# Value products of the prompt attention as two fp32r products of split operands, with the weighing on GpSimd

## The chip, the cores and the metric

The kernel runs on one core of a Trainium2 chip. The metric is the time of one execution on the device in microseconds (us); three executions of the kernel before took 1511.27, 1512.11 and 1513.88 us, the median is 1512.11.

TensorE is called PE in the profile, VectorE DVE, ScalarE ACT, GpSimd POOL and SyncE SP.

## The reference, cut to what matters

One layer of a decoder for a prompt of 1024 positions and, beside it, 8 x 4 sampled positions: a convolution, a pooling group and a sparse attention work side by side on 1024 features, then comes a feed-forward part. The change touches the attention of the prompt alone. It has 8 query heads in 2 groups (one key and value head per group, 64 features each) and three branches: compressed, selected and window, each with its own keys and values. For 1024 positions the selected branch comes down to all earlier positions; the window is 512 positions.

```python
    s = jnp.einsum('bqgrd,bgqmd->bgrqm', q, kg).astype(jnp.float32) * scale + bias
    p = masked_softmax(s, (dist >= 0)[:, :, None])
    o_slc = jnp.einsum('bgrqm,bgqmd->bqgrd', p.astype(vg.dtype), vg)
...
    p = masked_softmax(s, mask)
    o_win = jnp.einsum('bgrqk,bkgd->bqgrd', p.astype(vw.dtype), vw)
    return o_cmp, o_slc, o_win

def gate_sum(gates, o_cmp, o_slc, o_win):
    return gates[:, :, 0] * o_cmp + gates[:, :, 1] * o_slc + gates[:, :, 2] * o_win
```

All of it is fp32.

## The kernel before, in words

The program is one launch, with a hand-written instruction stream for every engine and semaphores between them. The stages follow each other: projection and convolution, the attention of the sampled positions, the attention of the prompt, output projection, feed-forward. The attention of the prompt runs from its first score product at 344.5 us to its last value product at 616.6 us.

There the work goes over 8 tiles of 128 queries (i = 0 to 7). Each tile has five groups in the order of the list ORDER: selected and window for the first head group (g = 0), the compressed branch for both, selected and window for the second (g = 1). A group of the selected or window branch is called dense; it has four heads (r = 0 to 3) and covers up to 1024 keys (selected) or 640 (window). The generator steps() sets the order of every engine: for each dense group q and each head r it yields the score jobs to issue and some of the turned tiles (128 keys, 4 heads) of the group three earlier (a lag of three groups). So the scores of one group, its exponentials, its weighing and its value products lie far apart in the program, and every engine walks the same list.

Of one step:

- TensorE makes the scores of a head into psA or psB (p_score, L1017 and L1018, fp32r, two products per 512 columns, one with the rounded queries and one with their rests). Then, per tile of the older group, it turns the weighed probabilities of four heads (four transposes of 128 x 128, L731) into a turn bank and makes the value product of the tile two before (p_values, L1037): an fp32 product of 512 columns into bank 6, whose 64 useful rows for g stand in one half, with zeros beside the values for the other half. Bank 6 collects all five groups of a query tile.
- VectorE adds the bias and takes the maximum of the job's scores (p_biased_max, L1814 to L1820), makes a group's four weights (reciprocal of the sum times the gate, group_weights, L1858 and L1861) once per group, and weighs one head of an older group (weigh_head, L1867: up to 1024 columns times one number per query, in place). The compressed branch has its own operations (c_center, L1834 and L1835; c_scale).
- ScalarE makes the exponentials of the jobs of the step before (L1415), copies every turned tile from its bank to probT (three slots, L1312), and copies bank 6 out to featT once per query tile (out_tile, L1421).
- GpSimd copies and pads the values of the prompt before the stage starts, and splits keys (L2143, L2144) and queries (L2146, L2150) into a rounded part and a rest, which the queue of SyncE copies to their places for the score products (L649).

The turned tiles go round three banks (4, 5, 7; turn_bank, turn_free): TensorE may turn tile u once tile u - 3 was copied out.

At the stage's end ScalarE copies out the last output (L1421), rounds the eight feature tiles (L1457), VectorE makes their rests (L1909), and TensorE goes on with the output projection (L1094). Rounded parts and rests of that projection's first two weight tiles are made before, at the tail of the attention (round_w on ScalarE, rest_w on VectorE, L1884).

Of the kernel before, what the change touches and what calls it, by code (L numbers as in the profile page):

```python
# [21 lines left out]
P = 128  # L22
D = 1024
# [220 lines left out]
def turn_bank(u):  # L244

    if U_C <= u < U_C + 2 * NB:
        return 4 + (u - U_C) % 4
    return 4 + u % 2 if u < U_T else (4, 5, 7)[(u - U_T) % 3]


def turn_free(u):

    if U_C <= u < U_C + 2 * NB:
        return u - 4 if u >= U_C + 4 else U_C - 1
    if U_C + 2 * NB <= u < U_C + 2 * NB + 2:
        return U_C + 2 * NB - 1
    return u - 2 if u < U_T else U_T - 1 if u < U_T + 3 else u - 3


OUT_AFTER = {i: max(u for k, u in PUNIT.items() if k[0] == "t" and GROUPS[k[1]][0] == i) for i in range(NT)}  # L260
# [23 lines left out]
def build(nc, A, out):  # L284
    ctx = ExitStack()
    with ctx:
# [84 lines left out]
        probT = [probTb[:, k, :] for k in range(NPT)]  # L371
        cmpw = at("cmpw", [P, 3, 8, P], 168960)
# [40 lines left out]
        def page_slot(pj, b):  # L413
# [39 lines left out]
            "gate_mm gate_ev qbd_done score_mm score_in exp_done sum_read cmp_scaled turn_drain_d probT_used keys_used out_done rec_done scaled o_ev v_pad split_done k_in q_in0 q_in1 q_in2 prob_zero "  # L453
            "x2_in0 x2_in1 x_pad mixH_done mixL_done raw_in0 raw_in1 wH_done wL_done unit_mm third_mm out_ev rest_ev "
            "acc_done moment_mm sd_done inv_done t_done silu_done up_scaled hid_done aH_done aL_done y_add gain2_in gain3_in "
# [17 lines left out]
        def wait_drained(eng, key):  # L473

            if key in DRAINED_D:
# [40 lines left out]
        def _(sp):  # L516
# [179 lines left out]
            def load_gu(f, w):  # L696
                if isinstance(f, int) and f == 1:
                    sp.wait_ge(s["acc_done"], 1)
                    sp.wait_ge(s["rest_ev"], 3 * KD)
                    sp.dma_start(gB[:, :], A["final_norm"][None, :].to_broadcast([P, D])).then_inc(s["gain3_in"], 16)  # L700
# [27 lines left out]
        def _(pe):  # L728
# [292 lines left out]
            def p_values(n, x):  # L1021

                i, g, br = GROUPS[n]
                pt = probT[PUNIT[("t", n, x)] % NPT]
                wait_drained(pe, ("t", n, x))
                o = bank[6]
                if br == 0:
                    mm = pe.matmul(o, vcBD, pt, start=False, stop=False)
                else:
                    first = x == 0 and (g, br) == ORDER[0]  # L1030
                    if first and i == 0:
                        pe.wait_ge(s["v_pad"], 4)
                    elif first:
                        pe.wait_ge(s["o_ev"], i)
# [172 lines left out]
        def _(sc_):  # L1207
# [224 lines left out]
            for _, _, jobs, tiles in steps():  # L1432
# [3 lines left out]
                for n, x in tiles:  # L1436
# [5 lines left out]
                    if key not in DRAINED_D:  # L1442
                        sc_.wait_ge(s["probT_used"], pu - NPT + 1)
                        drain(key, [(probT[pu % NPT], lambda b: b)])
                    else:
                        nturn[0] += 1
                    for o, last in OUT_AFTER.items():
                        if last == pu - 2:
                            out_tile(o)
            out_tile(NT - 1)  # L1450
# [3 lines left out]
            for k in range(KD):  # L1454
                if k == 4:
                    sc_.wait_ge(s["o_ev"], NT)
# [76 lines left out]
        def _(dve):  # L1533
# [335 lines left out]
            def turn_copy(key):  # L1869

                pu = PUNIT[key]
                dve.wait_ge(s["turn_fill"], UNIT[key] + 1)
                dve.wait_ge(s["probT_used"], pu - NPT + 1)
                dve.tensor_copy(probT[pu % NPT], bank[4 + UNIT[key] % 2]).then_inc(s["turn_drain_d"], 1)
# [12 lines left out]
            for q, r, jobs, tiles in steps():  # L1887
# [6 lines left out]
                if 0 <= old < len(DG):  # L1894
                    if head == 0:
                        group_weights(DG[old])
                    weigh_head(DG[old], head)
                if r == 3 and rider(q) is not None:
                    c_scale(rider(q))
                for n, x in tiles:  # L1900
                    if ("t", n, x) in DRAINED_D:
                        turn_copy(("t", n, x))
# [101 lines left out]
            dve.wait_ge(s["gain3_in"], 16)  # L2004
# [16 lines left out]
        def _(pool):  # L2021
# [213 lines left out]
```

## Time and profile before

| | |
|---|---|
| median of 3 executions | 1512.11 us (1511.27 to 1513.88) |
| the profiled execution | 1512.36 us |
| its span | 1510.2 us |
| mean granted TensorE clock of the span | 0.987 |
| TensorE / VectorE busy | 1451.0 / 759.1 us |
| ScalarE / GpSimd busy | 477.7 / 219.2 us |
| attention of the prompt | 344.5 to 616.6 us |

The span goes from the first to the last instruction of the profiled execution; the execution's own time is 2.2 us longer. Busy times of an engine are sums over its instructions' records; records of one engine overlap a little, since an instruction starts before the one ahead has left the pipeline. PEclk is the granted clock of TensorE in a stretch (1.00 is 2.4 GHz, 0.50 is 1.2 GHz). A line L731 stands for the operation that helper records, whatever the tile.

### The profile page before, as it was taken

What the parts mean: (1) busy time and instruction counts of PE and PEld (TensorE: products, weight loads), DVE (VectorE), ACT (ScalarE), POOL (GpSimd) and SP (SyncE); (2) the same over time, 40 slices, a digit from 0 to 9 for tenths busy, and PEclk for the clock granted to TensorE, in tenths of its full rate; (3) what the DMA queues carried; (4) which work ended last, traced back from release to release, by engine and by line L of the source; (5) the groups of instructions that cost most, each with busy time, mean ns of one, the idle gap of its engine ahead of it and who ended that gap; (6) DMA issues with size and microseconds to landing.
All of it is one profiled execution on the core that took longest, in us unless ns stands there. A gap on an engine that the chain in (4) does not pass through costs nothing.

```text
span 1510.2 us, 22117 instructions
## 1 busy us (share of the span) xinstructions
PE 1451.0 (96%) x8743; PEld 1330.9 (88%) x8743; DVE 759.1 (50%) x1535; ACT 477.7 (32%) x961; POOL 219.2 (15%) x251
## 2 busy tenths in 40 slices
PE   6999999888999999899999999999999999999996
PEld 6999988656666666699999999999999999999996
DVE  5499933226887776322424443524253344435257
ACT  5122124236776666422311211211121112111123
POOL 2114102520000000044220101010100101010105
PEclk9999999999999999999999999999999999999998
DMA  8731114943111102232110211202020202112012
GB/s 204 192 78 30 45 31 125 303 112 77 43 28 29 29 1 43 55 87 74 54 46 22 63 39 50 63 26 73 11 74 19 70 22 64 42 46 67 18 49 115
DMA packets 165815, 98.98 MB, mean 66 GB/s; under 512 B 35650, under 2 KB 160537, under 8 KB 165633
## 3 DMA queue, kind: packets, MB, share of 16 engines
q1 hardware_dynamic: 163217, 88.71, 21.5%
q0 software_dynamic: 2496, 8.88, 2.2%
q8 instruction: 69, 1.13, 0.3%
q14 instruction: 33, 0.27, 0.1%
HBM read 78.33 MB, written 13.19 MB: 61 GB/s over the span
## 4 chain that ended last, share of the span: by engine, by line
PE 82%; DVE 7%; SPq 3%; DMA 3%; ACT 2%; issue 2%; POOL 0%; POOLq 0%; DVEq 0%; ACTq 0%
PE psA L1065 16%; PE psB L1065 16%; PE psC L1065 16%; PE psD L1037 6%; PE psC L731 4%; DVE ybuf L1653 4%; DMA zraw<-in_w_in 2%; PE psD L731 2%; PE psA L782 2%; PE psA L1094 2%; PE psB L1094 2%; PE psC L1094 2%; PE psB L782 2%; PE psC L782 2%; PE psB L1017 1%
## 5 line engine op out<-in xcount | busy, mean ns | idle before, releaser
L1429 ACT CAST wH<-wraw 128x1024 fp32r<-128x1024 f32 (+1 forms) x132 | 86.7, 658 | 262.2 <-PE psC L1065 176.4
L2174 POOL TENSOR_TENSOR hid<-hid,rstdB 128x352 f32<-128x352 f32 x66 | 74.8, 1162 | 629.1 <-ACT hid L1490 629.1
L1037 PE MATMUL psD<-probTb,kvtok 128*128 128x512 f32 x264 | 135.7, 597 | 2.2 <-ACT featT L1421 2.1
L1884 DVE TENSOR_TENSOR wL<-wraw,wH 128x1024 fp32r<-128x1024 f32 (+1 forms) x132 | 107.2, 813 | 44.7 <-ACT wH L1429 44.7
L1065 PE MATMUL psA<-gH,wH 128*128 128x352 f32 x352 | 113.7, 323 | 0.0
L1065 PE MATMUL psB<-gH,wH 128*128 128x352 f32 x352 | 113.7, 323 | 0.0
L1065 PE MATMUL psC<-gH,wH 128*128 128x352 f32 x352 | 113.5, 322 | 0.0
L1065 PE MATMUL psA<-gH,wL 128*128 128x352 f32 x352 | 113.2, 322 | 0.0
L1065 PE MATMUL psB<-gH,wL 128*128 128x352 f32 x352 | 113.1, 321 | 0.0
L1065 PE MATMUL psA<-gL,wH 128*128 128x352 f32 x352 | 113.1, 321 | 0.0
L1065 PE MATMUL psB<-gL,wH 128*128 128x352 f32 x352 | 112.9, 321 | 0.0
L1065 PE MATMUL psC<-gL,wH 128*128 128x352 f32 x352 | 112.8, 321 | 0.0
L1065 PE MATMUL psC<-gH,wL 128*128 128x352 f32 x352 | 112.8, 320 | 0.0
L1653 DVE SCALAR_TENSOR_TENSOR ybuf<-glu,convw,ybuf 128x1296 f32<-128x1296 f32 x60 | 103.3, 1766 | 0.7
L1939 DVE TENSOR_TENSOR hid<-psA,rstdB 128x352 f32<-128x352 f32 x44 | 21.0, 520 | 160.7 <-PE psB L1065 160.6
L1947 DVE TENSOR_TENSOR hid<-psB,hid 128x352 f32<-128x352 f32 x22 | 11.5, 525 | 167.4 <-PE psC L1065 167.4
L1490 ACT ACTIVATE hid<-hid 128x352 f32<-128x352 f32 x66 | 29.9, 499 | 204.9 <-DVE hid L1939 204.9
L1312 ACT COPY probTb<-psC 128x512 f32<-128x512 f32 (+2 forms) x104 | 58.8, 565 | 46.7 <-PE psC L731 46.4
L1494 ACT CAST aH<-hid 128x352 fp32r<-128x352 f32 x66 | 31.5, 487 | 122.8 <-DVE hid L1947 121.8
L1065 PEld LDWEIGHTS psA<-gL,wH 128*128 128x128 f32 x352 | 66.4, 189 | 0.0
L1065 PEld LDWEIGHTS psB<-gH,wL 128*128 128x128 f32 x352 | 66.2, 188 | 0.0
L1065 PEld LDWEIGHTS psA<-gH,wH 128*128 128x128 f32 x352 | 66.0, 188 | 0.2
(426 smaller groups left out, 3898.7 us busy)
## 6 DMA issues: line engine op xcount, KB each, us to landing
wraw<-in_w_gu SPq DMA_DIRECT2D x44, 512.0 KB
wraw<-in_w_down SPq DMA_DIRECT2D x80, 128.0 KB
zraw<-in_w_in SPq DMA_DIRECT2D x12, 512.0 KB
xa<-in_x_prompt SPq DMA_DIRECT2D x8, 512.0 KB, 8.4
pages<-in_cache_cmp_kv SPq DMA_DIRECT2D x32, 128.0 KB, 2.4
qS<-qH SPq DMA_DIRECT2D x32, 128.0 KB, 2.4
qS<-qL SPq DMA_DIRECT2D x32, 128.0 KB, 2.4
xs<-in_x_prompt SPq DMA_DIRECT2D x8, 512.0 KB, 3.8
```

The lines of the kernel that those rows point to most:

```text
L731: return pe.transpose(dst, src, ident[0:n, 0:n])
L782: mm = pe.matmul(bank[3 * (m % 2) + n][:, 0:w], wt[:, m % 2, k, :], mv[:, k, c0:c0 + w], start=(k == 0 and wt is zH and mv is xH), stop=(k ...
L1037: mm = pe.matmul(o, kvtok[:, kt, vc:vc + P], pt, start=first, stop=((g, br) == ORDER[-1] and x == len(g_tiles(n)) - 1))
L1065: mm = pe.matmul(bank[3 * par + n][:, 0:cw], wt[:, par, k, :], mv[:, k, at:at + cw], start=(k == 0 and mv is mH and wt is wH), stop=(k == ...
L1094: mm = pe.matmul(b[:, 0:cw], wt[:, par, k, :], mv[:, k, c0:c0 + cw], start=False, stop=(k == KD - 1 and wt is wL))
L1312: op = sc_.copy(dst, srcfn(bank[turn_bank(u)]))
L1429: sc_.copy(wH[:, par, 0:nk, :], wraw[:, par, 0:nk, :]).then_inc(s["wH_done"], 1)
L1490: sc_.activation(hid[:, n, :], hid[:, n, :], ACT.Silu).then_inc(s["silu_done"], 1)
L1494: sc_.copy(aH[:, par, x // 2, at:at + cw], hid[:, n, :]).then_inc(s["aH_done"], 1)
L1653: op = dve.scalar_tensor_tensor(out=y, in0=x, scalar=w, in1=y, op0=ALU.mult, op1=ALU.add)
L1884: dve.tensor_tensor(wL[:, par, 0:nk, :], wraw[:, par, 0:nk, :], wH[:, par, 0:nk, :].bitcast(F32), ALU.subtract).then_inc(s["wL_done"], 1)
L2174: pool.tensor_tensor(hid[:, n, :], hid[:, n, :], rstdB[:, c0:c0 + cw], ALU.mult).then_inc(s["up_scaled"], 1)
```

## The change

It touches the value products and all that feeds them.

- The probabilities are kept as a rounded part and a rest: ScalarE's copy of a turned tile now rounds to fp32r (probH), and VectorE subtracts that from the bank (rest_tile, L1881: probL). TensorE's next turn into that bank, and the tile's value products, wait for this rest (semaphore pl_done).
- The values are split, too, by GpSimd: a tile vS holds for each key tile, branch and head group the 64 rounded columns and the 64 columns of rests side by side. One product with vS thus gives rounded and rest values in the two halves of the bank's rows. p_values makes two fp32r products per tile, with probH (L1048) and with probL (L1049).
- The outputs of g = 0 collect in bank 6 and those of g = 1 in bank 7, so there are two turn banks (4, 5) for the tiles. The compressed tile becomes two fp32 products over 64 rows each, one into bank 6 and one into bank 7.
- The two halves of a bank have to be added: ScalarE copies one half to featT (out_half, twice per query tile), VectorE adds the other (out_sum, L1889).
- The weighing of the probabilities moves from VectorE to GpSimd (L2184), group by group when the weights are there (rec_done).
- GpSimd's two padding copies and memsets of the values go; in their place stand 32 casts and 32 subtractions of 64 columns, each waiting for the one before, ahead of the split of the keys.
- Two semaphores are new (pl_done, o_half), one is folded into another (gain3_in into gain2_in).

```diff
@@ turn_bank, turn_free @@
-    return 4 + u % 2 if u < U_T else (4, 5, 7)[(u - U_T) % 3]
+    return 4 + u % 2
...
-    return u - 2 if u < U_T else U_T - 1 if u < U_T + 3 else u - 3
+    return u - 2
@@ wait_drained @@
+            if key in DENSE_T:
+                eng.wait_ge(s["pl_done"], DENSE_T[key] + 1)
@@ p_values @@
-                o = bank[6]
                 if br == 0:
-                    mm = pe.matmul(o, vcBD, pt, start=False, stop=False)
+                    if i:
+                        pe.wait_ge(s["o_ev"], 2 * i)
+                    pt = probT[slot]
+                    pe.matmul(bank[6], vcBD[0:HD, :], pt[0:HD, :], start=False, stop=False)
+                    mm = pe.matmul(bank[7], vcBD[HD:P, :], pt[HD:P, :], start=True, stop=False)
                 else:
...
-                    mm = pe.matmul(o, kvtok[:, kt, vc:vc + P], pt, start=first,
-                                   stop=((g, br) == ORDER[-1] and x == len(g_tiles(n)) - 1))
+                    last = br == 2 and x == len(g_tiles(n)) - 1
+                    pe.matmul(bank[6 + g], vS[:, kt, vc:vc + P], probH[:, slot, :], start=first, stop=False)
+                    mm = pe.matmul(bank[6 + g], vS[:, kt, vc:vc + P], probL[slot][:, :], start=False, stop=last)
@@ ScalarE @@
-            def out_tile(i):
-
-                sc_.wait_ge(s["probT_used"], OUT_AFTER[i] + 1)
-                sc_.copy(featT[:, 4:8, P * i:P * i + P], bank[6].rearrange("p (r t) -> p r t", r=GQ)
-                         ).then_inc(s["o_ev"], 1)
+            def out_half(i, g):
+
+                sc_.wait_ge(s["probT_used"], OUT_AFTER[i, g] + 1)
+                gp, other = slice(HD * g, HD * g + HD), slice(HD * (1 - g), HD * (1 - g) + HD)
+                sc_.copy(featT[gp, 4:8, P * i:P * i + P], bank[6 + g][other, :].rearrange("p (r t) -> p r t", r=GQ)
+                         ).then_inc(s["o_half"], 1)
...
-                        drain(key, [(probT[pu % NPT], lambda b: b)])
+                        drain(key, [(probH[:, pu % NPT, :] if n in DENSE else probT[pu % NPT], lambda b: b)])
@@ VectorE @@
-            def weigh_head(n, r):
-
-                p = prob(n, r)[:, 0:g_width(n)]
-                dve.tensor_scalar(p, p, precs[DENSE[n] % 4][:, r:r + 1], None, ALU.mult).then_inc(s["scaled"], 1)
...
+            def rest_tile(n, x):
+
+                key = ("t", n, x)
+                slot = PUNIT[key] % NPT
+                dve.wait_ge(s["turn_drain"], DRAINED_A[key])
+                dve.tensor_tensor(probL[slot][:, :], bank[turn_bank(UNIT[key])], probH[:, slot, :].bitcast(F32), ALU.subtract
+                                  ).then_inc(s["pl_done"], 1)
+
+            def out_sum(i, g):
+
+                gp = slice(HD * g, HD * g + HD)
+                o = featT[gp, 4:8, P * i:P * i + P]
+                dve.wait_ge(s["o_half"], 2 * i + g + 1)
+                dve.tensor_tensor(o, bank[6 + g][gp, :].rearrange("p (r t) -> p r t", r=GQ), o, ALU.add).then_inc(s["o_ev"], 1)
...
-                    weigh_head(DG[old], head)
...
+                    if n in DENSE:
+                        rest_tile(n, x)
+                    for o, last in OUT_AFTER.items():
+                        if last == PUNIT["t", n, x] - 4:
+                            out_sum(*o)
+            out_sum(NT - 1, 1)
             for w in range(2):
                 rest_w(w, w, KD)
@@ GpSimd @@
-            for br in (1, 2):
-                c = 256 * br
-                pool.tensor_copy(kvtok[:, 0:NT, c:c + HD], kvtok[:, 0:NT, c + P:c + P + HD]).then_inc(s["v_pad"], 1)
-            for br in (1, 2):
-                c = 256 * br
-                pool.wait_ge(s["v_pad"], br)
-                pool.memset(kvtok[:, 0:NT, c + HD:c + HD + P], 0.0).then_inc(s["v_pad"], 1)
...
+            for i in range(NT):
+                for br in (1, 2):
+                    c = 256 * br
+                    for g in range(KVH):
+                        v = kvtok[:, i, c + P + HD * g:c + P + HD * g + HD]
+                        vh = vS[:, i, c + P * g:c + P * g + HD]
+                        pad(pool.tensor_copy(vh, v))
+                        pad(pool.tensor_tensor(vS[:, i, c + P * g + HD:c + P * g + P], v, vh.bitcast(F32), ALU.subtract))
...
+            for q, n in enumerate(DG):
+                pool.wait_ge(s["rec_done"], q + 1)
+                for r in range(GQ):
+                    p = prob(n, r)[:, 0:g_width(n)]
+                    pool.tensor_scalar(p, p, precs[q % 4][:, r:r + 1], None, ALU.mult).then_inc(s["scaled"], 1)
```

The order of TensorE's instructions, before: one head of the last query tile, with two tiles of an older group (psC holds the turn banks 4 and 5, psD the banks 6 and 7; narrow and wide are the probabilities of window and selected groups).

```order
L1018 MATMUL psA<-kS,qS_111 128x320
L731 MATMUL psC<-cpk,wide 128x128 [waits turn_drain]
L731 MATMUL psC<-cpk,wide 128x128 x3
L1037 MATMUL psD<-probTb,kvtok 128x512 [waits turn_drain]
L731 MATMUL psC<-cpk,wide 128x128 [waits turn_drain]
L731 MATMUL psC<-cpk,wide 128x128 x3
L1037 MATMUL psD<-probTb,kvtok 128x512 [waits turn_drain]
L1017 MATMUL psB<-kS,qS_111 128x320 [waits exp_done]
```

And of the change, at the same place.

```order
L1025 MATMUL psA<-kS,qS_116 128x320
L738 MATMUL psC<-cpk,wide 128x128 [waits pl_done]
L738 MATMUL psC<-cpk,wide 128x128 x3
L1048 MATMUL psD<-probH,vS 128x512 [waits pl_done]
L1049 MATMUL psD<-probL_107,vS 128x512
L738 MATMUL psC<-cpk,wide 128x128 [waits pl_done]
L738 MATMUL psC<-cpk,wide 128x128 x3
L1048 MATMUL psD<-probH,vS 128x512 [waits pl_done]
L1049 MATMUL psD<-probL_105,vS 128x512
L1024 MATMUL psB<-kS,qS_116 128x320 [waits exp_done]
```

The places of transposes and value products are the same; both now wait for VectorE's rest (pl_done) where they waited for ScalarE's copy (turn_drain).

The order of VectorE's instructions in a step of the same stretch, before.

```order
L1814 TENSOR_TENSOR psB<-psB,tri 128x128 [waits score_mm]
L1818 TENSOR_REDUCE small_115<-psB 128x1 [waits dve]
L1820 ISA psB,nmax<-psB,btab,small_115 128x256 [waits exp_done,dve]
L1820 ISA nmax 128x1
L1867 TENSOR_SCALAR narrow<-narrow,small_115 128x640
```

And of the change.

```order
L1826 TENSOR_TENSOR psB<-psB,tri 128x128 [waits score_mm]
L1830 TENSOR_REDUCE small_120<-psB 128x1 [waits dve]
L1832 ISA psB,nmax<-psB,btab,small_120 128x256 [waits exp_done,dve]
L1832 ISA nmax 128x1
L1881 TENSOR_TENSOR probL_105<-psC,probH 128x512 [waits turn_drain]
L1881 TENSOR_TENSOR probL_106<-psC,probH 128x512 [waits turn_drain]
```

The weighing behind a maximum is gone, and the rests of the step's tiles (one or two) stand there, each waiting for ScalarE's copy.

VectorE at the end of the stage, before.

```order
L1861 TENSOR_TENSOR small_115<-small_115,kvtok 128x4 [waits sum_read]
L1867 TENSOR_SCALAR narrow<-narrow,small_115 128x640 [waits rec_done]
L1867 TENSOR_SCALAR narrow<-narrow,small_115 128x640 x3
L1884 TENSOR_TENSOR wL<-wraw,wH 128x1024 [waits wH_done] x2
L1909 TENSOR_TENSOR fL<-featT,fH 128x1056 [waits mixH_done] x8
```

And of the change.

```order
L1881 TENSOR_TENSOR probL_106<-psC,probH 128x512 [waits turn_drain]
L1881 TENSOR_TENSOR probL_107<-psC,probH 128x512 [waits turn_drain]
L1889 TENSOR_TENSOR featT<-psD,featT 64x4x128 [waits o_half]
L1899 TENSOR_TENSOR wL<-wraw,wH 128x1024 [waits wH_done] x2
L1927 TENSOR_TENSOR fL<-featT,fH 128x1056 [waits mixH_done] x8
```

The rests of the two weight tiles now stand behind the last tile's rest and the last half sum of the stage.

## Rows read from the trace of the kernel before

**Rows 1.** The page, busy times and shares of the span by engine:

```profile
PE 1451.0 (96%) x8743; PEld 1330.9 (88%) x8743; DVE 759.1 (50%) x1535; ACT 477.7 (32%) x961; POOL 219.2 (15%) x251
```

**Rows 2.** Windows of the stage (stretch, its length, busy by engine, PEclk, DMA share, GB/s):

```profile
371.80:588.90 217.10, 210.46 (x1042) 146.07 (x1042) 172.88 (x509) 149.51 (x319) 0.21 (x1) 1.00 0.10 25
588.90:616.60 27.70, 27.70 (x126) 16.20 (x125) 6.12 (x12) 14.13 (x25) 0.00 (x0) 1.00 0.29 58
```

**Rows 3.** Timeline of TensorE (start, us), and the page's group of value products:

```profile
542.67 0.40 PE L1018 MATMUL psB<-kS,qS 128*128 128x512 f32 x1
542.91 0.60 PE L731 MATMUL psD<-cpk,narrow 128*128 128x128 f32 x4
543.34 1.02 PE L1037 MATMUL psD<-probTb,kvtok 128*128 128x512 f32 x2
544.20 0.60 PE L731 MATMUL psC<-cpk,narrow 128*128 128x128 f32 x4
...
L1037 PE MATMUL psD<-probTb,kvtok 128*128 128x512 f32 x264 | 135.7, 597 | 2.2 <-ACT featT L1421 2.1
```

**Rows 4.** Timeline of VectorE, and the long part's window for L1867 alone (DVE busy):

```profile
559.92 0.69 DVE L1835 TENSOR_TENSOR psB<-psB,small 128x504 f32<-128x504 f32 x1
560.52 0.17 DVE L1858 RECIPROCAL small<-small 128x4 f32<-128x4 f32 x1
...
371.80:588.90 217.10, 50.92 (x95) 1.00 0.10 25
```

**Rows 5.** Timelines of GpSimd and SyncE's queue; groups of GpSimd by line:

```profile
290.03 1.89 POOL L2143 CAST keysH<-keysT 128x2048 fp32r<-128x2048 f32 x1
292.00 4.52 POOL L2144 TENSOR_TENSOR keysT<-keysT,keysH 128x2048 fp32r<-128x2048 f32 x1
296.47 3.59 POOL L2146 CAST qH<-qT 128x4096 fp32r<-128x4096 f32 x1
321.65 1.81 SPq L649 DMA_DIRECT2D kS<-keysH  x3
...
L2150 POOL TENSOR_TENSOR qL<-qT,qH 128x512 fp32r<-128x512 f32 x8 | 9.8, 1264 | 31.6 <-PE psD L974 31.6
L2174 POOL TENSOR_TENSOR hid<-hid,rstdB 128x352 f32<-128x352 f32 x66 | 74.8, 1162 | 629.1 <-ACT hid L1490 629.1
```

**Rows 6.** Timelines of TensorE and ScalarE in the tail:

```profile
588.72 0.60 PE L731 MATMUL psC<-cpk,wide 128*128 128x128 f32 x4
608.18 0.60 PE L731 MATMUL psC<-cpk,narrow 128*128 128x128 f32 x4
608.88 0.59 ACT L1312 COPY probTb<-psC 128x512 f32<-128x512 f32 x1 [0.71 <-PE psC L731]
613.38 0.60 PE L731 MATMUL psC<-cpk,narrow 128*128 128x128 f32 x4
```

**Rows 7.** The chain that ended last in order of time; VectorE's timeline:

```profile
616.59 0.59 ACT featT L1421
617.17 0.98 ACT fH L1457
618.18 9.46 DVE fL L1909 x8
627.68 0.79 PE psA L1094 x3
...
598.76 2.36 DVE L1884 TENSOR_TENSOR wL<-wraw,wH 128x1024 fp32r<-128x1024 f32 x2 [5.59 <-ACT wH L1429]
```

**Rows 8.** Windows around two low clocks (the first two: transposes alone, PE and PEld):

```profile
252.34:255.75 3.41, 3.41 (x16) 2.65 (x15) 0.50 0.80 229
255.75:270.00 14.25, 12.75 (x105) 11.05 (x103) 1.00 0.77 227
...
347.91:351.33 3.42, 2.04 (x14) 1.51 (x12) 3.00 (x20) 1.08 (x5) 0.00 (x0) 1.00 0.36 88
351.33:354.74 3.41, 2.83 (x13) 2.73 (x14) 2.98 (x22) 2.90 (x13) 0.00 (x0) 0.50 0.27 68
```

More of the change, by code:

```diff
@@ L256, in turn_free @@
         return U_C + 2 * NB - 1
-    return u - 2 if u < U_T else U_T - 1 if u < U_T + 3 else u - 3
-OUT_AFTER = {i: max(u for k, u in PUNIT.items() if k[0] == "t" and GROUPS[k[1]][0] == i) for i in range(NT)}
+    return u - 2
+OUT_AFTER = {(i, g): max(u for k, u in PUNIT.items() if k[0] == "t" and GROUPS[k[1]][:2] == (i, g))
+             for i in range(NT) for g in range(KVH)}
+DENSE_T = {k: m for m, k in enumerate([k for k in PUNIT if k[0] == "t" and k[1] in DENSE])}
 LASTQ = [(n, m) for n in range(3) for m in range(KD)]
@@ L371, in build @@
         probT = [probTb[:, k, :] for k in range(NPT)]
+        probH = at("probH", [P, NPT, 512], 158720, F32R)
+        probL = [at(f"probL{k}", [P, 512], o, F32R) for k, o in enumerate((54528, 164864, M_S + 2528))]
+        vS = at("vS", [P, NT + 1, KVG], M_Z, F32R)
         cmpw = at("cmpw", [P, 3, 8, P], 168960)
@@ L452, in build @@
             "late_zero turn_fill turn_drain page_in0 page_in1 page_in2 page_in3 cmpw_in0 cmpw_in1 cmpw_in2 cmpw_used cmp_half cmp_sum cmp_ev posr_in "
-            "gate_mm gate_ev qbd_done score_mm score_in exp_done sum_read cmp_scaled turn_drain_d probT_used keys_used out_done rec_done scaled o_ev v_pad split_done k_in q_in0 q_in1 q_in2 prob_zero "
+            "gate_mm gate_ev qbd_done score_mm score_in exp_done sum_read cmp_scaled turn_drain_d probT_used keys_used out_done rec_done scaled pl_done o_half o_ev v_pad split_done k_in q_in0 q_in1 q_in2 prob_zero "
             "x2_in0 x2_in1 x_pad mixH_done mixL_done raw_in0 raw_in1 wH_done wL_done unit_mm third_mm out_ev rest_ev "
-            "acc_done moment_mm sd_done inv_done t_done silu_done up_scaled hid_done aH_done aL_done y_add gain2_in gain3_in "
+            "acc_done moment_mm sd_done inv_done t_done silu_done up_scaled hid_done aH_done aL_done y_add gain2_in "
             "lraw_in0 lraw_in1 lH_done lL_done last_mm y_last back_turn x_add sq_y accf_done ms3 rstd3 y_done_d y_done_a y_out").split()
@@ L473, in wait_drained @@
         def wait_drained(eng, key):
-            if key in DRAINED_D:
+            if key in DENSE_T:
+                eng.wait_ge(s["pl_done"], DENSE_T[key] + 1)
+            elif key in DRAINED_D:
                 eng.wait_ge(s["turn_drain_d"], DRAINED_D[key])
@@ L1448, in _ @@
                         if last == pu - 2:
-                            out_tile(o)
-            out_tile(NT - 1)
+                            out_half(*o)
+            out_half(NT - 1, 1)
             sc_.wait_ge(s["stores"], 16 * STORES)
@@ L1455, in _ @@
                 if k == 4:
-                    sc_.wait_ge(s["o_ev"], NT)
+                    sc_.wait_ge(s["o_ev"], 2 * NT)
                 sc_.copy(fH[:, k, :], featT[:, k, :]).then_inc(s["mixH_done"], 1)
@@ L1862, in group_weights @@
                 dve.wait_ge(s["rec_done"], q + 1)
-            def weigh_head(n, r):
-                p = prob(n, r)[:, 0:g_width(n)]
-                dve.tensor_scalar(p, p, precs[DENSE[n] % 4][:, r:r + 1], None, ALU.mult).then_inc(s["scaled"], 1)
[L1869 to L1874, printed above, removed]
+            def rest_tile(n, x):
[9 more added lines that the diff above has]
+                dve.tensor_tensor(o, bank[6 + g][gp, :].rearrange("p (r t) -> p r t", r=GQ), o, ALU.add).then_inc(s["o_ev"], 1)
             def link2(op):
@@ L2002, in last_scale @@
                                       ).then_inc(s["y_done_d"], 1)
-            dve.wait_ge(s["gain3_in"], 16)
+            dve.wait_ge(s["gain2_in"], 32)
             for q, turns in last_steps():
@@ L2140, in in_turn, with pad @@
                 pool.wait_ge(s["pool"], count[0])
+            pads = [0]
+            def pad(op):
+                pads[0] += 1
+                op.then_inc(s["v_pad"], 1)
+                pool.wait_ge(s["v_pad"], pads[0])
+            for i in range(NT):
[6 more added lines that the diff above has]
+                        pad(pool.tensor_tensor(vS[:, i, c + P * g + HD:c + P * g + P], v, vh.bitcast(F32), ALU.subtract))
             old = slice(0, T)
```

12 lines of the change are left out of this document (5 added, 7 removed).

## The prediction

> **What bounds the kernel now.** The page's busy shares come first: TensorE is busy 96% of the span and VectorE 50% [rows 1], so an edit that only shortens VectorE would be worth nothing on average. But these are averages over the whole program, and the change touches one stage, so the windows come next. The attention of the prompt runs from 344.5 us (first score product) to 616.6 us (last value product). In its long part, 371.8 to 588.9 us, TensorE is busy 210.46 of 217.10 us and VectorE 172.88 [rows 2]: TensorE is the bound, VectorE follows at 80%. The 27.7 us after that hold no scores, only the last three groups' tiles: TensorE is busy throughout, VectorE for 6.12 us. Then come 11 us in which TensorE waits for the rests of the features [rows 7]. GpSimd does nothing in the stage but one memset. So I read two limits: what TensorE gives back, and how close VectorE is behind it.
>
> **What a tile costs TensorE.** In the timeline four transposes start at 542.91 and the value product behind them at 543.34: 0.43 us. The next transposes start at 544.20: the fp32 value product, which the trace shows as two passes of 512 columns, holds TensorE for 0.86 us. A score product, fp32r with 512 columns, starts at 542.67 and the next instruction at 542.91: 0.24 us [rows 3]. The change puts two fp32r products of 512 columns where one fp32 product was: 2 x 0.24 = 0.48 instead of 0.86, 0.38 us less per tile. There are 132 tiles of the selected and window branches (x264 passes), so 50 us less for TensorE, 114 x 0.38 = 43 us of it in the long part: 210.5 - 43 = 167 us of work there. The compressed tiles (8) become two products of 64 rows each; even at twice 0.86 they add 7 us to an engine that then has 40 us to spare. I cost them at nothing.
>
> **What VectorE gets.** Removed: the weighing, 95 instructions and 50.92 us of records in the long part. Records overlap: an operation of 504 columns from PSUM starts at 559.92, is recorded with 0.69 us, and the next one starts at 560.52, 0.60 later [rows 4]. With 0.08 us of overlap each, the weighing frees 50.9 - 95 x 0.08 = 43 us. Added: one subtraction per tile (128 x 512, PSUM minus SBUF), nearest to that row of 504 columns, so 0.605 us of the queue: 114 x 0.605 = 69 us, and the two half sums of each query tile, same form, 14 x 0.605 = 8.5 us. VectorE in the long part: 172.9 - 43 + 69 + 8.5 = 207.4 us. That is more than TensorE's 167: **VectorE becomes the bound**, and of the 43 us that TensorE gives back at most 217.1 - 207.4 = 9.7 can show. What remains is idle time of VectorE. TensorE, as the bound with three turn banks, was idle 217.1 - 210.5 = 6.6 us. Now there are two turn banks, a bank comes free only when VectorE has subtracted, and a subtraction at the head of VectorE's queue holds back the next score's maximum. Against that, ScalarE (some 150 us of the long part, plus eight half copies) and TensorE have 50 and 40 us of slack. I take 5 us of idle, between 0 (gain 9.7) and 10 (gain nothing): **-4.7 us**. The short first part (344.5 to 371.8, small tiles, waiting on each other rather than on throughput) gets one more link per tile: +0.5.
>
> **GpSimd.** It takes over the weighing. The trace has no such operation there. From below: a cast of 2048 columns took 1.89 us, 0.92 ns a column; from above: a product of two inputs in the feed-forward part, 352 columns in 1162 ns, 3.3 ns a column [rows 5]. The widest query tile (four groups, 8 x 1024 + 8 x 640 = 13,312 columns) then costs 12 to 44 us of GpSimd per some 45 us, and its result is wanted nearly two groups later. One input is nearer to the cast, so I take 0.92 and cost it at nothing; the cover is the lag of three groups. The Trainium skill's GPSIMD Engine Reference (§ 4.1 Engine selection) calls GpSimd about two times slower than VectorE for operations of two inputs and roughly line-rate for one; the two rows agree with that, and it points to the lower end.
>
> GpSimd also splits the values into 64 small casts and subtractions that wait on each other, ahead of the keys' split, in place of two copies and two memsets. Casts of 2048 and 4096 columns took 1.89 and 3.59 us, so 0.19 fixed and 0.83 ns a column: 0.25 us for 64 columns; subtractions of 512 and 2048 columns took 1.26 and 4.52, so 0.32 for 64. With 0.08 between dependent ones (the cast that starts 290.03 and ends 291.92, the next at 292.00) it is 32 x (0.33 + 0.40) = 23 us. The keys' split ended at 296.5 and would end at 320; the DMA queue asks for it at 321.65, after its own wait for TensorE [rows 5]. Hidden, by 2 us.
>
> **The tail.** Now the first transposes of the part start at 588.72 and the last at 613.38, 19 steps of 1.30 us, and the end comes 3.2 us later [rows 6]. After the change TensorE needs 0.43 + 0.48 = 0.91, but the ring through two banks is longer: transposes 0.60, ScalarE's start 0.10 behind (608.78 to 608.88), its copy 0.59, 0.10, subtraction 0.69, 0.10: 2.18 us for two tiles, 1.09 each. So 19 x 1.09 + 2.18 + 0.67 (last two products and their drain) = 23.6 against 27.9: **-4.3 us**.
>
> **The end of the stage.** From 616.59 the chain is: copy of the last output 0.59, rounding of the features, their rests on VectorE 9.46, and TensorE goes on at 627.68 [rows 7]. In the new order of VectorE the last half sum stands ahead of the rests of the first two weight tiles (2.36 us, now done at 598.76 in the idle tail), and these ahead of the feature rests. So 0.59 + 0.05 + 0.69 + 0.05 + 2.36 + 0.05 + 9.46 = 13.2 instead of 11.1: **+2.1 us**.
>
> **Sum.** -4.7 + 0.5 - 4.3 + 2.1 = -6.4 us. The profiled execution took 1512.36 us (span 1510.2), 0.25 above the median of 1512.11; against the median this gives 1505.7.
>
> **Rivals.**
> *VectorE runs packed* (chance 0.08): the rests fall into its idle time, no more is lost than semaphores. For: VectorE's records already lie close in narrow steps. Gain 9.7 + 4.3 - 2.1 = 12: 1500.
> *Half the gain is lost to the ring* (0.15): 10 us of idle instead of 5, and a ring of 1.15: 1510 to 1513, no change.
> *VectorE's queue is blocked* (0.10), the case on the other side: in 22 steps of the long part two tiles stand behind one maximum. If the second subtraction there waits for one copy of ScalarE (0.59), since its bank came free only with the subtraction before, that is 13 us: 1505.7 + 13 = 1519. It decides from 0.3 us per such step (6.6 us) on. Against it: while the maximum runs (over 1 us), the copy of the first tile and the transposes of the second fit in.
> *GpSimd is late with the keys* (0.06): at over 0.39 us per small operation (25 us / 64) the key copies move. At 0.62 they start 15 us late, some 5 of which the queue's slack before the first score takes: 1516.
> *GpSimd is late with the weights* (0.03): only above 3.5 ns a column; at 4, 270 us for all 67,584 columns, over 1520.
> *The clock falls* (0.03). TensorE will be busy for 80% of the long part, a good part of it transposes. In the trace it went to 0.50 (1.2 GHz) at 351.33 after 2.04 busy of 3.42 us; and in 252.34:255.75, at 0.50, every record is a transpose, and the stretch behind it has 1.00 [rows 8]. So transposes did not keep the clock down. If it fell for every other such stretch, TensorE would need 167 x 4/3 = 223 instead of 212: 1516. The Trainium skill (TensorE: Matmul & The Clock Gate, Part 4) says that transposes do not count as busy in the same way; by that rule this rival would be likely, but rows 8 speak against it.
>
> **How the numbers follow.** The forecast, 1502 to 1509, has 0.55. A measurement of this kernel tells about 0.2% (3 us) from no change. Faster by more: 0.55 + 0.08 = 0.63. Within: 0.15 and a little of the keys' case, 0.17. Slower: 0.20. The range 1500 to 1516.5 takes in the first three cases and those of the keys and the clock, both 1516; it leaves out 0.13 above and a little below.
>
> **What would show it.** Right: value products at two starts 0.24 apart; TensorE at about 80% and VectorE at over 95% in the long part; waits of TensorE for the subtraction; tiles at 1.09 in the tail; two weight rests between last half sum and feature rests; GpSimd's weighing near 1 ns a column. Wrong: VectorE waiting for ScalarE's copies for more than 10 us in the long part, the first score later than 345 us, TensorE's clock at 0.50 beyond 360 us, or scaled probabilities waited for.

## The result, and the profile after

The changed kernel took 1525.45 us (median of 4 runs, 1524.9 to 1528.06) against 1512.84 for the kernel before (4 runs): a ratio of 1.0088, interval 1.007 to 1.0105. It is 13 us slower, where 6 us faster was forecast; the time lies above the range. The profiled execution took 1525.53 us, its span is 1523.7. One execution of the run with the memset on VectorE (3898.55 us) and one of the kernel before beside it (2074.16) lie far off and are left out of the medians below.

The page's first part of the kernel after answers to [rows 1]: TensorE is busy 31 us less, GpSimd 217 us more.

```profile
PE 1419.9 (93%) x8759; PEld 1328.0 (87%) x8759; DVE 798.9 (52%) x1555; ACT 481.5 (32%) x969; POOL 436.2 (29%) x439
```

The windows of the kernel after answer to [rows 2] (stretch, its length, busy PE, PEld, DVE, ACT, POOL, each with its count, then PEclk, DMA share, GB/s). The first line is the long part; the next two lie in the tail.

```profile
371.80:588.90 217.10, 184.15 (x1044) 143.85 (x1044) 200.13 (x529) 149.87 (x319) 169.15 (x95) 0.98 0.09 23
...
599.80:615.26 15.46, 0.00 (x0) 0.00 (x0) 0.74 (x2) 3.33 (x5) 3.36 (x3) 0.63 0.48 103
615.26:620.45 5.19, 5.18 (x19) 4.29 (x20) 2.52 (x4) 2.06 (x4) 0.00 (x0) 0.50 0.01 3
```

In the tail TensorE stands still for 15.46 us, and for the 5.19 us behind that it runs at the lower clock (0.50). The chain that ended last, of the kernel after in order of time, tells what the pause waits for:

```profile
595.57 7.44 POOL narrow L2184 x4
603.01 0.16 POOL xs L2186
...
603.23 0.37 SPq L680
...
607.98 0.60 SPq L696
608.58 0.04 issue
608.62 4.31 DMA wraw<-in_w_out
...
613.91 0.59 ACT probH L1323
614.49 0.02 issue
614.52 0.70 DVE probL L1881
```

GpSimd finishes the last group's weighing at 603.0; only then comes its memset of the padding rows of the output projection's input (xs). The queue of SyncE waits for that memset before it loads xs, the gain and the first two weight tiles, in this order. The two weight tiles have landed at about 610.8 and 612.9. ScalarE has their rounding (L1441) in its queue ahead of the last two groups' copies, so the copies wait, VectorE's rest behind them, and TensorE's next turn behind that. ScalarE's timeline of the kernel after shows the gap:

```profile
597.29 0.59 ACT L1323 CAST probH<-psC 128x512 fp32r<-128x512 f32 x1 [0.69 <-PE psC L738]
610.86 1.04 ACT L1441 CAST wH<-wraw 128x1024 fp32r<-128x1024 f32 x1 [12.98 <-DMA wraw<-in_w_out]
612.96 1.04 ACT L1441 CAST wH<-wraw 128x1024 fp32r<-128x1024 f32 x1 [1.05 <-DMA wraw<-in_w_out]
```

In the kernel before the same load was issued right behind the last score product (SyncE's timeline of before):

```profile
587.93 0.37 SPq L673 DMA_DIRECT2D xs<-in_x_prompt  x1
```

So the account of the stage, from the two profiled executions: the first score product starts at 343.89 (344.84 before), the last one at 587.25 (587.27): nothing gained up to there. From there to the end of the value products it takes 43.5 us (587.25 to 630.77) instead of 29.3 (587.27 to 616.57): 14.2 more. From there to the last rest of the features 13.1 (to 643.83) instead of 11.1 (to 627.64): 2.0 more. Together 16.2. The span is 13.5 us longer; the other 2.7 come back behind the stage, where the change alters no work. That stretch took 882.6 us before and 879.9 after, and between 878.2 and 881.6 in the runs below, so this part is not put down to the change.

### The profile page after: what moved, and what is told of

It is laid out like the page before. It is cut to its first block, busy times and chain, and to the rows that moved or that the text cites. A ratio compares the mean times of both kernels' runs of the same rounds, so it can differ in the third digit from the quotient of the medians.

```text
span 1523.7 us, 22397 instructions
## 1 busy us (share of the span) xinstructions
PE 1419.9 (93%) x8759; PEld 1328.0 (87%) x8759; DVE 798.9 (52%) x1555; ACT 481.5 (32%) x969; POOL 436.2 (29%) x439
## 4 chain that ended last, share of the span: by engine, by line
PE 76%; DVE 12%; issue 4%; ACT 3%; DMA 2%; POOL 2%; SPq 1%; POOLq 0%; DVEq 0%; ACTq 0%
PE psA L1076 16%; PE psB L1076 16%; PE psC L1076 15%; PE psA L789 4%; PE psB L789 4%; PE psC L789 4%; PE psC L738 3%; DVE small L1830 3%; DVE probL L1881 2%; PE psA L1105 2%; PE psC L1105 2%; PE psB L1105 2%; DVE ybuf L1665 1%; PE psD L738 1%; DVE psB L1832 1%
## 5 line engine op out<-in xcount | busy, mean ns | idle before, releaser
L1441 ACT CAST wH<-wraw 128x1024 fp32r<-128x1024 f32 (+1 forms) x132 | 86.8, 658 | 272.5 <-PE psC L1076 174.0
L2184 POOL TENSOR_SCALAR wide<-wide,small 128x128 f32<-128x128 f32 (+7 forms) x64 | 109.3, 1726 | 33.9 <-DVE small L1873 33.9
L1881 DVE TENSOR_TENSOR probL<-psC,probH 128x512 fp32r<-128x512 f32 x132 | 89.3, 688 | 34.3 <-ACT probH L1323 33.2
L2184 POOL TENSOR_SCALAR narrow<-narrow,small 128x640 f32<-128x640 f32 (+4 forms) x64 | 93.9, 1487 | 25.6 <-DVE small L1873 25.6
L1323 ACT CAST probH<-psC 128x512 fp32r<-128x512 f32 x132 | 76.6, 583 | 38.1 <-PE psC L738 37.3
L738 PE MATMUL psC<-cpk,wide 128*128 128x128 f32 x320 | 51.7, 287 | 22.5 <-DVE probL L1881 22.4
```

The costliest lines, as they stand in the source:

```text
L738: return pe.transpose(dst, src, ident[0:n, 0:n])
L1323: op = sc_.copy(dst, srcfn(bank[turn_bank(u)]))
L1441: sc_.copy(wH[:, par, 0:nk, :], wraw[:, par, 0:nk, :]).then_inc(s["wH_done"], 1)
L1881: dve.tensor_tensor(probL[slot][:, :], bank[turn_bank(UNIT[key])], probH[:, slot, :].bitcast(F32), ALU.subtract).then_inc(s["pl_done"], 1)
L2184: pool.tensor_scalar(p, p, precs[q % 4][:, r:r + 1], None, ALU.mult).then_inc(s["scaled"], 1)
```

## The experiments

Theory Q: the place of one memset in GpSimd's queue makes the pause. Rivals: the weights come late for another reason, or GpSimd's price itself ends the tail. Theory D: VectorE's throughput bounds the long part; its rival R: the ring of two banks does. The medians of the kernel before in the three sets of runs are 1512.24 (first four), 1513.31 (next four) and 1512.67 (the last).

**The memset on VectorE.**

```diff
-            pool.wait_ge(s["score_mm"], NSJ + NJ)
-            pool.memset(xs[0][:, NT, :], 0.0).then_inc(s["x_pad"], 1)
...
+                if (q, r) == (len(DG) - 1, GQ - 1):
+                    dve.memset(xs[0][:, NT, :], 0.0).then_inc(s["x_pad"], 1)
```

> The change as it is, but the one memset that the loads of the output projection's first input and weights wait for is issued by VectorE behind its last maximum, and no longer by GpSimd behind the last weighing. Theory Q (the 15.5 us in which TensorE stands still at 599.8 to 615.3 come from the place of that memset in GpSimd's queue): memset near 588 instead of 603, the weight tiles land near 598, ScalarE's rounding of them no longer holds up the copies of turned tiles, and the slow clock behind the pause goes, too: 1509 us (1507 to 1511). Rival W (the weights come late for a reason of their own, or ScalarE would wait there anyway): the pause stays for the most part, 1518 or more. Rival P (GpSimd's price of 3 ns a column is itself what ends the tail): TensorE then waits for the last group's weighing instead, 1515 to 1520.

Measured: 1513.31 us, ratio 1.0011 (1.0001 to 1.002), 12 us less than the change. Most of the pause is gone and the time lies below what W and P gave, so both fall. 4 us more than expected stay, and VectorE's timeline of this run shows why:

```profile
591.01 0.17 DVE L1909 MEMSET xs<- 128x128 f32 x1
```

And ScalarE's timeline of this run:

```profile
600.79 1.04 ACT L1441 CAST wH<-wraw 128x1024 fp32r<-128x1024 f32 x1 [1.03 <-DMA wraw<-in_w_out]
```

On VectorE the memset has work ahead of it, too, and comes 3 us after the last score product. ScalarE still waits 1.03 us for the second tile, TensorE then 2.40 for the rest behind it, and the low clock follows again.

**The two weight rests off the chain.**

```diff
+            rest_w(0, 0, KD)
             out_sum(NT - 1, 1)
-            for w in range(2):
-                rest_w(w, w, KD)
...
                                   ).then_inc(s["mixL_done"], 1)
+            rest_w(1, 1, KD)
```

> The run before this one, and besides the rest of the first weight tile is made ahead of the last half sum, that of the second behind the rests of the features. The chain behind the last value product then holds no weight rest (2.36 us in the trace of the change): 2.3 us less than the run with the memset alone, about 1507 us. If the two rests were hidden, no difference.

Measured: 1511.05 us, ratio 0.9994 (0.9984 to 1.0004): 2.3 us less than the run before. The time misses the 1507 by the 4 us that were left there; the difference is the one expected. The chain that ended last, of the change:

```profile
631.38 0.69 DVE featT L1889
632.07 0.03 issue
632.10 2.36 DVE wL L1899 x2
634.46 9.36 DVE fL L1927 x8
```

And of this run:

```profile
619.90 0.58 ACT featT L1433
620.50 1.08 ACT fH L1469
621.60 9.45 DVE fL L1928 x8
```

The half sum and the weight rests are no longer on it. This term was forecast as it came out.

**One part alone: the kernel before, with the weighing on GpSimd.**

```diff
-                    weigh_head(DG[old], head)
...
+            for q, n in enumerate(DG):
+                pool.wait_ge(s["rec_done"], q + 1)
+                for r in range(GQ):
+                    p = prob(n, r)[:, 0:g_width(n)]
+                    pool.tensor_scalar(p, p, precs[q % 4][:, r:r + 1], None, ALU.mult).then_inc(s["scaled"], 1)
             pool.wait_ge(s["score_mm"], NSJ + NJ)
             pool.memset(xs[0][:, NT, :], 0.0).then_inc(s["x_pad"], 1)
```

> The kernel before with one part of the change alone: the weighing on GpSimd, ahead of its memset, as the change has it; value product, banks and outputs as before. Theory Q: the long part is bound by TensorE and keeps its length, but the memset comes behind the last weighing, at about 600 instead of 588, so the weights land near 610 where ScalarE wants them near 598: a pause of about 12 us in the tail, 1524 us (1520 to 1527). If the pause comes from the new value products or from the ring of two banks, it isn't here: 1509 to 1513.

Measured: 1524.39 us, ratio 1.0071 (1.0057 to 1.0085). The old value products, three banks, and the same loss. ScalarE's timeline of this run:

```profile
607.07 1.04 ACT L1429 CAST wH<-wraw 128x1024 fp32r<-128x1024 f32 x1 [11.78 <-DMA wraw<-in_w_out]
```

**The same with the memset on VectorE** (the edit of the first run).

> The run before this one with the memset on VectorE behind its last maximum. Theory Q: no pause, and since TensorE bounds the long part, taking 43 us of weighing off VectorE brings next to nothing: 1511 us (1508 to 1513). If GpSimd's weighing at 3 ns a column is late for TensorE's turns, over 1515.

Measured: 1506.19 us, ratio 0.9967 (0.9954 to 0.998). The memset's place alone is worth 18 us between these two runs. And the weighing on GpSimd brings 5 to 6 us by itself, more than expected: from the first score product to the last it takes 238.1 us (345.89 to 584.01) instead of 242.4 (344.84 to 587.27). In the window from 371.8 to the last score product's end, below, TensorE is idle for 3.6 of 212.5 us, where it was for 6.6 of 215.8 up to the same product before (371.8 to 587.58). Of TensorE's waits from 371.8 to 584 two are gone, 2.1 us for ScalarE's copy of bank 6 and 1.1 us for exponentials of selected groups. VectorE is busy for only 133.31 us here; that its queue had held these up before is likely, but not shown.

```profile
371.80:584.30 212.50, 208.91 (x1039) 145.47 (x1038) 133.31 (x412) 148.81 (x318) 171.55 (x98) 1.00 0.10 26
```

**The change with the weighing undone.**

```diff
                     if head == 0:
                         group_weights(DG[old])
+                    wn = DG[old]
+                    wp = prob(wn, head)[:, 0:g_width(wn)]
+                    dve.tensor_scalar(wp, wp, precs[old % 4][:, head:head + 1], None, ALU.mult).then_inc(s["scaled"], 1)
...
-            for q, n in enumerate(DG):
-                pool.wait_ge(s["rec_done"], q + 1)
...
```

> The change with the weighing alone undone (VectorE weighs again, GpSimd's memset then has nothing ahead of it), the two weight rests moved off the chain as in the run with memset and rests, and ScalarE's rounding of the second weight tile one group later. Theory D (VectorE's throughput bounds the long part of the change): 43 us of weighing come on top of 199 us of busy VectorE in 216 us: the long part takes 240 to 250 us, the run 1533 to 1545 us. If VectorE were not the bound (the ring of two banks is), under 1520.

Measured: 1545.53 us, ratio 1.0217 (1.0195 to 1.0238), just above the end of what theory D gave and far from the 1520 of its rival. The window of this run from 371.8 to 621.6 shows VectorE busy for 238.72 of 249.80 us. The last score product ends 3.3 us later, at 624.91, so the long part takes 253.1 us, 3 more than the 250 that were the upper end.

```profile
371.80:621.60 249.80, 193.38 (x1042) 147.60 (x1041) 238.72 (x630) 151.83 (x325) 0.00 (x0) 0.95 0.09 22
```

**The memset early on GpSimd, and the second weight tile rounded later** (the weight rests are moved as in the second run, and the memset behind the weighing is taken out; the cut shows the two new parts).

```diff
             for q, n in enumerate(DG):
+                if q == len(DG) - 2:
+                    for u in range(2 * NT - 3, 2 * NT):
+                        pool.wait_ge(s[f"q_in{u % 3}"], 64 * (u // 3 + 1))
+                    pool.memset(xs[0][:, NT, :], 0.0).then_inc(s["x_pad"], 1)
                 pool.wait_ge(s["rec_done"], q + 1)
...
                     if (n, x) == (NG - 2, 0):
-                        for w in range(2):
-                            round_w(w, w, KD)
+                        round_w(0, 0, KD)
+                    if (n, x) == (NG - 1, 0):
+                        round_w(1, 1, KD)
```

> The change with the memset still on GpSimd, but ahead of the last two groups' weighing (it waits for the last query copies alone), the two weight rests off the chain, and ScalarE's rounding of the second weight tile one group later. Theory Q: loads start with the last score product, no pause is left in the tail (2.4 us and a slow clock behind it were left with the memset on VectorE, where it stood at 591.0): 1507 us (1505 to 1509). If the pause is not the queue's, as the run with memset and rests: 1511.

Measured: 1508.03 us, ratio 0.9964 (0.9951 to 0.9978). This is the change without its mishap, 17 us below it, and 5.3 us below the kernel before. In its trace the tail, from the last score product's start to the end of the value products, takes 26.5 us (591.42 to 617.89), and TensorE's longest wait in it is 0.75 us.

**VectorE relieved, the ring untouched.**

```diff
                 if w > m:
                     least = far[:, job % 2:job % 2 + 1]
-                    link(dve.tensor_reduce(least, sc[:, 0:w - m], AX, ALU.min))
+                    least = 3.0e38
```

> The run with the early memset, and VectorE leaves out the maximum over the keys farther than 256 (95 instructions, some 45 us of its queue in the long part; the exponentials then have a bias from the near keys alone). Nothing of the ring of turned tiles changes. Theory D (throughput): VectorE has 155 us of work left, TensorE 181, the long part goes from 216 to 185-195: 1476 to 1490 us. Theory R (the ring of two banks with the subtraction in it sets the pace): the long part keeps its length within some us, over 1500.

Measured: 1484.76 us, ratio 0.9809 (0.979 to 0.9829), 23 us less than the run with the early memset. It is a probe of VectorE's time and no kernel to keep, since the exponentials lose the maximum over the far keys. The window of this run from 371.8 to the last score product's end:

```profile
371.80:567.80 196.00, 174.31 (x1046) 142.97 (x1046) 152.03 (x440) 150.70 (x325) 171.56 (x99) 1.00 0.11 28
```

And of the run with the early memset:

```profile
371.80:591.70 219.90, 183.63 (x1051) 142.09 (x1049) 201.78 (x535) 151.78 (x326) 171.84 (x100) 0.99 0.10 25
```

VectorE has 49.8 us less to do and the stretch is 23.9 us shorter (1 us above the 185 to 195 expected), with the same two banks. Theory R falls as the cause of the long part's length; the ring is not free either, since only half of what VectorE gave back shows, and now VectorE is idle for 44 us, 30.2 of them in waits for ScalarE's copies of turned tiles. One rival is left open: the run also shortens the way from a job's scores to its exponentials, so by itself it doesn't part VectorE's throughput from that latency. The run with the weighing undone, which adds work behind the maxima and not between scores and exponentials, speaks for throughput.

**Half the tiles split, then two of three.** A tile that is not split keeps its probabilities in fp32 and has no subtraction:

```diff
-DENSE_T = {k: m for m, k in enumerate([k for k in PUNIT if k[0] == "t" and k[1] in DENSE])}
+DENSE_T = {}
+for _j, _k in enumerate([k for k in PUNIT if k[0] == "t" and k[1] in DENSE]):
+    if _j >= 112 or _j % 2:
+        DENSE_T[_k] = len(DENSE_T)
...
+                    else:
+                        mm = pe.matmul(bank[6 + g], vS[:, kt, vc:vc + P].bitcast(F32), probT[slot], start=first, stop=last)
```

> The run with the early memset, but every second tile of the first 112 is not split: its probabilities are copied in fp32 and go through one fp32 product with the same side-by-side values; its subtraction falls away. The last 20 tiles are all split. Theory D: VectorE in the long part 199 - 56 x 0.605 = 165 us, TensorE 181 + 56 x 0.38 = 202: TensorE bounds again, long part 203 to 206 instead of 216: 1495 us (1492 to 1500). If neither VectorE nor TensorE is the bound (GpSimd's weighing, say), 1504 or more.

> The run with half the tiles split, with two of three tiles split among the first 112 (19 more). Theory D: TensorE 200 - 19 x 0.38 = 193 us, VectorE 176 + 19 x 0.605 = 187 us in the long part: nearly level, so the larger falls by 7 us, but both are then close to full and wait for each other: 0 to 5 us less than with half split, 1498 to 1503 us. If VectorE is already the one that waits are made by, more than with half split, up to 1508.

Measured: 1503.47 us, ratio 0.9937 (0.9923 to 0.9951), for half, 3.5 us above its range; the profiled execution of that one was its fastest, 1499.34. 1500.62 us, ratio 0.9924 (0.9907 to 0.994), for two thirds (_j % 3), within its range. The intervals of the two overlap, so which of them is better stays open; both beat the kernel before and the change. The window to the last score product's end, with half:

```profile
371.80:582.10 210.30, 194.67 (x1046) 143.85 (x1045) 172.22 (x477) 149.96 (x321) 169.43 (x97) 0.99 0.10 25
```

And with two thirds:

```profile
371.80:584.00 212.20, 191.93 (x1052) 143.80 (x1050) 184.03 (x500) 152.07 (x325) 171.72 (x100) 0.99 0.10 26
```

The exchange is as the terms say (TensorE down, VectorE up), but the stretch stays at 210 to 212 us, above the 203 to 206 expected of half. Neither engine is full (TensorE is idle for 15.6 and 20.3 us, VectorE for 38 and 28); which of their waits sets the length was not taken apart.

These windows all begin at 371.8, while the first score product starts between 343.9 and 346.4 us in the profiled executions. Counted from the first score product's start to the last one's, the part takes 242.4 us before, 243.4 after, 238.1 with the weighing alone on GpSimd and the memset on VectorE, 245.6 with the early memset (345.81 to 591.42; this execution was the slowest of its run), 237.9 with half split (343.99 to 581.84) and 237.6 with two thirds (346.13 to 583.69). The last score products of the weighing alone and of the run with the early memset:

```profile
584.01 0.31 PE L1018 MATMUL psB<-kS,qS 128*128 128x320 f32 x1
591.42 0.31 PE L1025 MATMUL psB<-kS,qS 128*128 128x320 f32 x1
```

So beside the weighing alone the split of all tiles lengthens this part by 5 to 7 us, and the split of some of them hardly changes it. What the split gives is the tail: 29.3 us before and with the weighing alone, 26.5 with all tiles split and the early memset, 25.6 and 25.8 with half and two thirds. On balance the whole change with the early memset (ratio 0.9964) is no faster than the weighing alone (0.9967).

## Why the prediction was wrong, point by point

**The step that failed is the one on GpSimd**: "I take 0.92 and cost it at nothing; the cover is the lag of three groups". The cover held for those who wait for the weighing itself: TensorE's weight loads waited 1.1 us in all for GpSimd in the stage. But the cover was checked for the weighing alone. What stands behind it in GpSimd's queue, the memset, has a waiter of its own, SyncE's queue of loads, and behind those ScalarE's rounding stands in the queue of the copies. The prediction had read that "GpSimd does nothing in the stage but one memset" [rows 2] and didn't ask who waits for that. The answer was 15.46 us in which TensorE stood still. Shown by the run with the weighing alone (the pause without the new products), most cleanly by its pair, 1524.39 and 1506.19, in which the memset's place alone differs, and by the three places of the memset in the change: 1525.45 behind the weighing, 1511.05 on VectorE (with the weight rests moved), 1508.03 early (with those, and the second weight tile's rounding later). The last link, the rounding in ScalarE's queue ahead of the copies, is read from the program and the traces; no run moved the rounding by itself and left the memset where it was.

**GpSimd's price** was taken near the lower bound and came out near the upper one. Groups by line and shape, GpSimd after:

```profile
L2184 POOL TENSOR_SCALAR narrow<-narrow,small 128x640 f32<-128x640 f32 x32 | 59.8, 1888 | 16.6 <-DVE small L1873 16.6
L2184 POOL TENSOR_SCALAR wide<-wide,small 128x1024 f32<-128x1024 f32 x8 | 22.6, 2848 | 5.1 <-DVE small L1873 5.1
...
L2184 POOL TENSOR_SCALAR wide<-wide,small 128x128 f32<-128x128 f32 x8 | 4.7, 604 | 8.4 <-DVE small L1873 8.4
```

And for the same 640 columns VectorE before:

```profile
L1867 DVE TENSOR_SCALAR narrow<-narrow,small 128x640 f32<-128x640 f32 x28 | 15.4, 551 | 0.2
```

1888 ns for 640 columns are 2.95 ns a column, 203 us for all, where 0.92 was taken from the cast. The Trainium skill's GPSIMD Engine Reference (§ 4.1 Engine selection), which pointed to the lower end, differs from this row: GpSimd takes 3.4 times as long as VectorE here, with one tensor input and a number per row. A cast was the wrong neighbour; the product of two inputs (3.3 ns) was the right one. Nor did the two rows bear out "about two times slower" as closely as the prediction says: 3.3 ns against VectorE's 1.2 (504 columns in 0.60 us [rows 4]) is 2.75 times. The price lengthened the pause: the last group's weights were there at 595.05, and its four weighings began at 595.57, behind those of the group before; with 0.92 they would have ended near 598 instead of 603, an estimate from these rows; the memset would still have been 10 us later than before. That was not tried.

**The long part** (-4.7 forecast, and +0.5 for the short first part; together, from the first score product's start to the last one's, +0.9 came). VectorE's work was sized well: 200.13 us busy after, 207.4 forecast. TensorE's was too low: 184.15 (181.58 in the same stretch of the first run, at a clock of 1.00) where 167 was forecast; the first product of a pair holds TensorE 0.32 us (540.35 to 540.67), not 0.24, which is 9 us for 114 tiles; the remainder was not taken apart. What failed is "I take 5 us of idle": 217.1 - 200.1 is 17 us. The waits of VectorE in the long part of the kernel after (who waits, for whom: us in all, times, longest):

```profile
DVE probL L1881 <- ACT probH L1323: 4.2, 12, 0.9
DVE small L1830 <- PE psA L1025: 1.4, 2, 0.8
```

And the longest of TensorE's in the same view:

```profile
PE psC L738 <- DVE probL L1881: 16.1, 18, 2.0
```

Named waits make up 9.6 us of the 17 (all rows of that view together); the rest is in no row, and VectorE's timeline shows gaps of some 0.04 us between dependent instructions (one record ends at 586.54, the next starts at 586.58). The 4.2 us for ScalarE's copies also answer the rival "VectorE's queue is blocked", which needed over 6.6. So the part came out like the rival "half the gain is lost to the ring", whose 10 us of idle were too few, too; but the ring alone is not what sets its length (run without the far maximum). "VectorE becomes the bound" was right: taking work off VectorE shortens the part, putting work on (weighing undone) lengthens it.

**The tail** (-4.3 forecast). Without the pause it would have been: 43.5 us less 15.5, less about 1.9 for the slow clock (an estimate: 5.2 us at 0.50 for three tiles, that take 3.3 at 1.09) is 26.1 against 29.3: about -3.1. The run with the early memset, with no such pause, measures it: 26.5, -2.8. The rate of 1.09 a tile fits: the transposes start at 620.45, 621.53, 622.68, 623.68, 624.80.

**The end** (+2.1 forecast): +2.0 in the trace, and 2.3 in the run that takes it away. Right, with the order of VectorE's queue read before the run.

**The values' split and the keys**: 0.24 and 0.32 us for the small operations were forecast at 0.25 and 0.32; the keys were ready at 317, the loads weren't late, the first score product was 0.95 us earlier. Right. **The clock** averaged 0.98 in the long part, but one sign of being wrong, "TensorE's clock at 0.50 beyond 360 us", did show: in three short stretches, from 371.8, 392.3 and 440.1 us on, it was 0.52 to 0.53. That cost nothing that can be seen: in the run with the memset on VectorE it was 1.00 in the whole long part, VectorE's idle time is the same 17 us (199.81 busy of 217.1), and first to last score product take 243.8 us against 243.4. So the rival of the falling clock, which needed it in every other stretch, did not come about. What the clock did cost came in the tail, behind the pause.

Without the memset's mishap the change is worth -5.3 us (the run with the early memset, with the weight rests moved, too). The terms forecast for that are -4.7 + 0.5 - 4.3 = -8.5. The weighing alone, with the memset moved, gives as much, so splitting all the value products brought nothing on balance: the long part lost what the tail gained.

## What to carry to other kernels

When work is put on an engine that had nearly none, list what that engine already has to issue behind it, however small, and follow each item's waiters through the other queues: a memset of 0.2 us cost TensorE 15 us, by way of the queues of SyncE and ScalarE. A resource that two engines can pay for (here fp32 on TensorE or a subtraction on VectorE) need not be paid by one for all tiles; when a third to a half of the tiles kept the old way, the long part came back to what it takes with no tile split (238 us), and the tail kept its gain. And an average price per column is taken from the operation of the same kind of operands, not from the nearest shape.

## What was not expected of the hardware

GpSimd's product of a tile with one number per row took 604 ns for 128 columns and 2848 for 1024: 2.5 ns for each column further, as slow as its operations on two tiles. For 640 columns it took 1888 ns in the change and 1887 with the weighing alone and the memset on VectorE, where VectorE was far less busy (133 us of the long part instead of 200), so no effect of VectorE's load on it shows. And the granted clock of TensorE was 0.50 (1.2 GHz) for 5.2 us behind a pause of 15.5 us, which made it 0.77 us from the first transpose of a tile to its product (615.26 to 616.03), and 0.41 later (624.80 to 625.21).
